# Feed-forward input of a float32 decoder block: product results added onto seeded PSUM banks, and two of four k groups in four column chunks

## The reference

```
h = rms_norm(x, ffn_pre_gain)                    # 256 x 2048
gt, up = split(h @ w_ffn_in)                     # w_ffn_in: 2048 x (2 x 5632)
x = x + rms_norm((silu(gt) * up) @ w_ffn_out, ffn_post_gain)
```

## Time and profile before

| | before |
|---|---|
| median of 3 runs | 1494.03 us (1493.93 to 1494.49) |
| profiled execution, span from first to last instruction | 1491.6 us |
| PE busy | 1481.7 us, 99% |
| DVE busy | 1137.2 us, 76% |
| ACT busy | 835.4 us, 56% |
| weight blocks loaded | 530, 512 KB each |

### The profile page before, as it was taken

One profiled execution on the slowest core, in us unless ns is written; L12 is line 12 of the kernel. 1 busy time (PEld: TensorE's weight loads), 2 busy tenths in 40 slices (PEclk: granted clock), 3 DMA queues, 4 the chain that ended last, 5 costly groups with the idle time before them and its releaser, 6 DMA issues.

```text
span 1491.6 us, 19212 instructions
## 1 busy us (share of the span) xinstructions
PE 1481.7 (99%) x6712; PEld 1220.6 (82%) x6712; DVE 1137.2 (76%) x1353; ACT 835.4 (56%) x1018; POOL 151.4 (10%) x286
## 2 busy tenths in 40 slices
PE   9999999999999999999999999999999999999997
PEld 7888887888888888888888888888888888888886
DVE  6878988855554577657576788888888888887897
ACT  6645455565666544656678455555555555555554
POOL 0000000140220000000000221012222221100000
PEclk9999999999999999999999999999999999999999
DMA  9755555565555655856463666766666667656564
GB/s 342 235 186 178 182 180 186 189 208 187 188 192 171 239 183 185 334 195 211 161 197 116 198 209 221 230 212 216 209 212 199 198 217 236 231 173 213 187 208 169
DMA packets 89859, 305.08 MB, mean 205 GB/s; under 512 B 13056, under 2 KB 13568, under 8 KB 88768
## 3 DMA queue, kind: packets, MB, share of 16 engines
q1 hardware_dynamic: 80144, 285.12, 57.6%
q0 software_dynamic: 9216, 18.63, 3.9%
q10 hardware_dynamic: 432, 0.45, 0.1%
HBM read 294.19 MB, written 2.10 MB: 199 GB/s over the span
## 4 chain that ended last, share of the span: by engine, by line
PE 99%; DMA 0%; DVE 0%; SPq 0%; ACT 0%; issue 0%; DVEq 0%
PE acc L1808 10%; PE acc L1809 10%; PE acc L1810 10%; PE acc L2128 5%; PE acc L2131 5%; PE acc L2130 5%; PE side L2130 5%; PE side L2131 5%; PE side L2128 5%; PE side L1808 4%; PE side L1809 4%; PE side L1810 4%; PE tr L1808 3%; PE tr L1809 3%; PE tr L1810 3%; PE side L2093 2%
## 5 line engine op out<-in xcount | busy, mean ns | idle before, releaser
L548 ACT ACTIVATE w_hi<-raw 128x1024 fp32r<-128x1024 f32 x299 | 315.1, 1060 | 295.4 <-PE acc L2131 90.2
L1001 DVE TENSOR_TENSOR w_lo<-raw,w_hi 128x1024 fp32r<-128x1024 f32 x262 | 320.9, 1227 | 202.0 <-ACT w_hi L529 197.7
L1006 DVE TENSOR_TENSOR w_lo<-raw,w_hi 128x1024 fp32r<-128x1024 f32 x315 | 381.5, 1222 | 102.8 <-ACT w_hi L548 92.9
L529 ACT ACTIVATE w_hi<-raw 128x1024 fp32r<-128x1024 f32 x262 | 276.9, 1059 | 281.3 <-PE acc L1810 165.6
L1808 PE MATMUL acc<-w_hi,xT_hi 128*128 128x512 f32 x504 | 198.3, 393 | 0.5 <-DVE w_lo L1001 0.5
L1810 PE MATMUL acc<-w_hi,xT_lo 128*128 128x512 f32 x504 | 196.3, 389 | 0.0
L1809 PE MATMUL acc<-w_lo,xT_hi 128*128 128x512 f32 x504 | 196.3, 389 | 0.0
L503 POOL DMA_DIRECT2D hT_st<-h_blk x176 | 93.6, 540 | 492.1 <-DVE h_blk L1073 453.6
L1808 PEld LDWEIGHTS acc<-w_hi,xT_hi 128*128 128x128 f32 x504 | 94.6, 188 | 22.6 <-issue 2.6
L1810 PEld LDWEIGHTS acc<-w_hi,xT_lo 128*128 128x128 f32 x504 | 94.6, 188 | 20.0
L1809 PEld LDWEIGHTS acc<-w_lo,xT_hi 128*128 128x128 f32 x504 | 94.7, 188 | 18.9
(11 more groups left out here) (468 smaller groups left out, 2747.3 us busy)
## 6 DMA issues: line engine op xcount, KB each, us to landing
raw<-in_units SPq DMA_DIRECT2D x530, 512.0 KB, 3.9
hT_st<-h_blk POOLq DMA_DIRECT2D x176, 32.0 KB, 1.8
x_tok<-in_x SPq DMA_DIRECT2D x4, 512.0 KB, 5.9
qkT<-qk_blk POOLq DMA_DIRECT2D x64, 32.0 KB, 2.9
xres<-in_x POOLq DMA_DIRECT2D x1, 2048.0 KB, 11.0
m_raw<-in_mem_t POOLq DMA_DIRECT2D x1, 2048.0 KB, 8.6
mq<-in_mem POOLq DMA_DIRECT2D x1, 2048.0 KB, 15.4
x_raw<-in_x_t SPq DMA_DIRECT2D x6, 256.0 KB, 6.4
```

Source lines behind the costliest of these rows:

```text
L529: a_.activation(w_hi[:, j % RING], raw[:, j % RING], ACT.Copy).then_inc(hi_ready, 1)
L548: a_.activation(w_hi[:, v % RING], raw[:, slots[block]], ACT.Copy).then_inc(hi_ready, 1)
L1001: v_.tensor_tensor(w_lo[:, s], raw[:, s], w_hi[:, s].bitcast(F32), ALU.subtract).then_inc(lo_ready, 1)
L1006: v_.tensor_tensor(lo[:, v % RING], raw[:, slot], hi[:, v % RING].bitcast(F32), ALU.subtract).then_inc(lo_ready, 1)
```

## The change

Only the feed-forward input changes (and the numbering of the units behind it: its units are now 280 to 485 and the end is at 595).

- **Pairs per body**: `PAIRS`, 1, 2, 1, 2, 1, 2, 1, 2, 1, 1 for bodies 1 to 10.
- **Order within a body**: block products come first, with three plain up units of the chunk before between them; then that chunk's other up units, and then the body's plain gate units. Chunk 0's last four up units go into body 1.
- **Seeded banks**: products are added by PE onto banks that already hold a partial sum. ACT copies the first product (gate bank 0) into up bank 1, later the sum in up bank 1 into gate bank 1; DVE adds the copy `e_sb` of the second product to up bank 1, once into up bank 0 and once in place. Gate and up results then stand complete in four banks that alternate between two sets from body to body, and silu and the hidden product read them there.
- **Slots**: `raw`'s four slots get four more (`EARLY_SLOTS`, in the place of parts of `hT` not yet written) and two for bodies 2 to 8 (`GROUP_SLOTS`), whose first loads wait for `s_lo` = 2, the second set of activation sums. That set is made in body 1, at its first gate unit.
- **Differences** (`sums`) may be made one or more steps ahead of the product that uses them.

The names of a body's steps: B11, B12, B22, B21 are weight blocks, T1 to T4 the differences of them, in the order made. With two pairs a and b each product step is doubled. Body 4 is units 338 to 361: B11a, B11b, up, T1a, T1b, B21a, B21b, T2a, T2b, up, T3a, T3b, B22a, B22b, up, T4a, T4b, then 3 up and 4 gate units. A one-pair body is B11, up, T1, B21, T2, up, T3, B22, up, T4, and then the other units.

```diff
+PAIRS = (0, 1, 2, 1, 2, 1, 2, 1, 2, 1, 1)
+    rest = [("up", 0, j) for j in range(4, CU)]
+    for i in range(1, 11):
+        k = [[("block", i, g, n) for n in range(4)] for g in range(b.p)]
+        for g in range(b.p):
+            step(k[g][B11])
+        b.p1 = now()
+        t1 = [total(k[g][B11], k[g][B12], k[g][B11], now()) for g in range(b.p)]
+        step(rest[0], 0, t1)
+        for g in range(b.p):
+            step(k[g][B11], t1[g][4])
+        b.p5 = now()
+        t2 = [total(k[g][B11], k[g][B22], k[g][B11], now()) for g in range(b.p)]
+        for g in range(b.p):
+            step(k[g][B21], 0, t2 if g == 0 else ())
+        for g in range(b.p):
+            step(k[g][B11], t2[g][4])
+        b.p6 = now()
+        t3 = [total(k[g][B12], k[g][B22], k[g][B12], 0) for g in range(b.p)]
+        step(rest[1], 0, t3)
+        t4 = [total(k[g][B11], k[g][B21], k[g][B11], b.p6) for g in range(b.p)]
+        for g in range(b.p):
+            step(k[g][B12], t3[g][4], t4 if g == 0 else ())
+        b.p7 = now()
+        for g in range(b.p):
+            step(k[g][B22])
+        step(rest[2])
+        for g in range(b.p):
+            step(k[g][B11], t4[g][4])
...
@@ sync @@
+                elif slot < RING + EARLY_SLOTS:
+                    sp_.wait_ge(x2_ready, 8)
+                else:
+                    sp_.wait_ge(s_lo, 2)
@@ scalar: the loop over a body's splits @@
+                    if v == b.first and i > 1:
+                        gate_silu(i - 1)
+                    if v == b.p1 - 1:
+                        act.wait_ge(unit_used, b.p1)
+                        a_.activation(up_bank(i, 1), gate_bank(i, 0), ACT.Copy).then_inc(u2_seeded, 1)
+                    if v == b.p5 - 1:
+                        a_.activation(e_sb[:], gate_bank(i, 1), ACT.Copy).then_inc(p5_copied, 1)
+                    if v == b.p7 - 1:
+                        a_.activation(gate_bank(i, 1), up_bank(i, 1), ACT.Copy).then_inc(gate1_seeded, 1)
+                    if v == b.blocks - 1 and i > 1:
+                        hidden_hi(i - 1)
+                    if v == b.blocks and i == 1 and max(PAIRS) > 1:
+                        s_hi_part(1)
+                    split_late(v + RING)
@@ vector: the loop over a body's splits @@
+                    if v == b.p6 - 1:
+                        dve.wait_ge(unit_used, b.p6)
+                        dve.wait_ge(p5_copied, i)
+                        v_.tensor_tensor(up_bank(i, 0), up_bank(i, 1), e_sb[:], ALU.add).then_inc(up0_seeded, 1)
+                    if v == b.p7 + 1:
+                        dve.wait_ge(gate1_seeded, i)
+                        v_.tensor_tensor(up_bank(i, 1), up_bank(i, 1), e_sb[:], ALU.add).then_inc(up1_seeded, 1)
+                    if v == b.blocks:
+                        if i > 1:
+                            hidden_lo(i - 1)
+                        hidden_product(i - 1)
+                        if i == 1 and max(PAIRS) > 1:
+                            x_sums(1)
+                    if v == b.blocks + 2:
+                        if i == 1 and max(PAIRS) > 1:
+                            x_sums_lo(1)
+                        hidden_turn(i)
+                    split_late(v + RING)
@@ tensor: the loop over bodies @@
+                for g in range(b.p):
+                    late_product(v + g, gates_[0], *x_block(g, 0, 0), g == 0)
+                if i > 1:
+                    pe.wait_ge(up1_seeded, i - 1)
+                late_unit(v, before, b.up[0][2])
+                pe.wait_ge(s_lo, b.p)
+                for g in range(b.p):
+                    late_product(v + g, gates_[1], *sum_of(S_hi[g], S_lo[g], 0), g == 0)
+                pe.wait_ge(u2_seeded, i)
+                for g in range(b.p):
+                    late_product(v + g, gates_[0], *x_block(g, 1, 0), False)
+                for g in range(b.p):
+                    late_product(v + g, ups[1], *sum_of(S_hi[g], S_lo[g], 1), False)
+                late_unit(v, before, b.up[1][2])
+                pe.wait_ge(up0_seeded, i)
+                for g in range(b.p):
+                    late_product(v + g, ups[1], *sum_of(S_hi[g], S_lo[g], 2), False)
+                for g in range(b.p):
+                    late_product(v + g, ups[0], *sum_of(S_hi[g], S_lo[g], 3), False)
+                late_unit(v, before, b.up[2][2])
+                pe.wait_ge(gate1_seeded, i)
+                for g in range(b.p):
+                    late_product(v + g, gates_[1], *x_block(g, 1, 1), False)
...
```

More of the change, by code:

```diff
@@ L60 @@
 G_S5, G_PRE, G_PROJ, G_MID, G_GLU, G_GATE, G_BR, G_OUT, G_MK, G_XQ, G_MV, G_XO, G_FI, G_FO = (
-    0, 1, 4, 12, 13, 15, 23, 35, 39, 40, 41, 42, 46, 68)
+    0, 1, 4, 12, 13, 15, 23, 35, 39, 40, 41, 42, 46, 47)
 T_GLU, T_BR, T_X1 = 0, 2, 10
-FI_SPLITS, FO_SPLITS, FO_LAST = 19, 53, 56
-S_FI, S_FO, S_END = 284, 474, 583
-def late_units():
[L69 to L80, removed]
-        for _ in range(count):
[L82 to L100, removed]
@@ L101, in late_units @@
     for count in (12, 8, 4):
-        plain(count)
-        pair()
-    plain(8)
+        out_plain(count)
+        out_pair()
+    out_plain(8)
     for count in (4, 8, 4, 4):
[L106 to L119, removed]
+        out_plain(count)
+        out_pair()
+    out_plain(8)
+    first, last = {}, {}
@@ L122 @@
+    plan = {}
+    for n, (key, t, sums) in enumerate(steps):
+        plan[S_FI + n] = place[key] + (t, [tuple(place[k] for k in a[:3]) + a[3:] for a in sums])
+    return loads, plan, bodies, s_fo, now()
+LATE_LOADS, LATE_STEPS, BODIES, S_FO, S_END = late_units()
 N_X, N_GM, N_Y1, N_MEM, N_X1, N_Y2, N_X2, N_Y3 = range(8)
@@ L929, in ffn_in @@
[L929 to L944, removed]
@@ L949, in _ @@
+            for v in range(BODIES[9].end, S_FO):
+                if v == BODIES[9].end:
+                    gate_silu(10)
+                split_late(v + RING)
             preload(3, ACT.Sqrt)
@@ L2148, in out_plain @@
+            pe.wait_ge(up1_seeded, 10)
+            for j in range(2 * BODIES[9].p, CU):
+                late_unit(BODIES[9].end + j - 2 * BODIES[9].p, [up_bank(10, h) for h in range(HALVES)], j)
             def out_plain(q, count, n, g, begins=(None, None), last=False):
@@ L2234 @@
             k0, k1 = 2 * plain[2 * g], 2 * plain[2 * g + 1]
-            order += [left[k0:k1], right[k0:k1]] + blocks_of(left, right, g)
-        order += [left[2 * end:], right[2 * end:]]
+            outs += [left[k0:k1], right[k0:k1]] + blocks_of(left, right, g)
+        outs += [left[2 * end:], right[2 * end:]]
+    for n, block in enumerate(_np.concatenate(outs)):
+        late["out", n] = block[None]
+    order += [late[key] for key, slot, splits in LATE_LOADS]
     def turned(a):
```

359 lines of the change are left out of this document (222 added, 137 removed).

## The result

| | before | changed |
|---|---|---|
| median | 1494.17 us (4 runs) | 1524.01 us (4 runs, 1522.75 to 1525.42) |
| profiled execution, span | 1491.6 us | 1520.8 us |
| PE matmuls | 6712 | 6688 |

The ratio is 1.0199, with a 95% interval of 1.0185 to 1.0214: slower by 29.8 us, where 22 were forecast; 1524.01 lies in the range of 1504 to 1526.

The account below looks back on a forecast made before the run. PE's matmul count was taken as the bound, with DVE's queue setting the pace in dense stretches. Dense bodies 18.0, one-pair bodies 4.0, body 2's one-off 5.2, less 5.4 saved, gave +21.8 us: 1516 us, range 1504 to 1526.

Parts of the forecast that it names:

- The path and its cover: Whole kernel: the path is PE's matmul count at 0.2267 us each while splits arrive in time, with 0.6 us to spare.
- The saving: Feed-forward bodies: four more pairs, each replacing 48 matmuls by 42, take 5.44 us off PE.
- Dense bodies: Two-pair bodies: PE loses 4.51 us each ahead of T3 in three waits; four such bodies, 18.0 us.
- Split to difference 1.26: DVE queue: a difference starts 1.26 us after the start of the split before it.
- Difference to the next 1.27: DVE queue: a difference starts 1.27 us after the start of the difference before it.
- One-pair bodies: Bodies 3, 5, 7, 9 and 10: PE reaches T3 0.80 us late in each, 4.0 us in all.
- Body 2: Body 2: loads held for the second activation sums add 5.2 us to its own 4.5, making 9.7 us.
- Body 1: Body 1: no silu before it, so it loses nothing.
- The output part: Output part: old plan of splits and loads, with the last body's sums off DVE; nothing changes there.
- The spreading works: Rival, bodies: plain units between products let DVE regain its lead, PE never waits; 1488.6 us, chance 0.08.
- No change: Rival, dense bodies: waits of about 1.3 us each eat the gain; 1494 us, chance 0.04.
- The clock: Rival: granted clock falls to 1.2 GHz after each dense body's long wait, adding 10.9 us; 1526.8 us, chance 0.08.

Follow-up runs that it names:

- two spread kernels that move the differences: Changed kernel with later group slots, up units spread wider and differences made at the last up unit before their product: 1489.23 us; also without a difference's subtrahend wait: 1488.87 us.
- later group slots: Changed kernel with the plan taking the two group slots only from unit 295 on, so body 2's first blocks take other slots: 1516.72 us.
- two traces with one wait fewer: Changed kernel, and the spread kernel with moved differences, each without a difference's wait for its subtrahend's landing: 1524.40 us and 1488.87 us.
- spread only: Changed kernel with up units spread wider (2, 2, 2 in two-pair bodies; 2, 1, 1 in body 1) and group slots later, differences not moved: 1499.67 us.
- the seed twice: Changed kernel with DVE making the add that seeds up bank 0 twice in each body: 1535.78 us.
- later silu: Changed kernel with ACT's two silu halves moved from a body's first step to one step after T3: 1522.74 us.

## Why the prediction was right, and where it was off

**The path and its cover.** Right: PE bounds the kernel while the splits arrive in time, and the dense products use that time up. The changed kernel's PE keeps its 0.2267 us outside the waits, and taking the differences off DVE restores it (the run without them).

**The saving.** Right: -5.4 by count, and -4.8 and -5.2 in the two spread kernels that move the differences, with no wait of PE left in the bodies.

**Dense bodies.** Right in mechanism and place; 4.87 against 4.51, and bodies 3 and 4 together took 88.63 us, 5.7 over the 82.96 where 5.3 was said. The three waits (0.42, 1.24, 2.36 in brackets; by the starts about 0.7, 1.5 and 2.6) are the forecast 0.4, 1.5, 2.6. Two steps of the chain were mis-sized. "Split to difference 1.26" stands in it once ahead of a held difference and is now 1.42 (0.20 idle in the rows above): a difference stands behind four semaphore waits and not two, of which one is for the split just before it; with one of the others removed the step is 1.31. "Difference to the next 1.27" stands in it three times and was misread: the earlier trace rows have 886.18 - 884.85 = 1.33, and the changed kernel's rows have 1.35 and 1.36. Together that is 0.4 us a dense body.

**One-pair bodies.** Right, 0.79 against 0.80. That ACT's silu is part of this chain is shown by the run that moved it.

**Body 2.** The mechanism is right (later group slots take 8.2 us away), the size was 9.7 against 13.1. Two terms fell short. The waits themselves took 10.8: at the body's head PE lost 0.7 and not 1.9, but the fifth load of the burst, put at 10.3 us after the first issue by the median landing and 1.49 us a load, was later. The landings of the burst ran to 15.2 us at most, and the difference that needs this load began at 866.37, 12.2 us after the issue at 854.19. The other term is the clock: the rival that was held at 0.08 for every dense body came true here, once, for 2.4 us. A granted clock below 1.00 was among the signs named for being wrong; it did not touch the other bodies of this execution.

**Body 1.** "Body 1 has no silu before it and loses nothing" is the step that failed. ACT is busy until 812.9 with the squares of the norm, loads an activation table from 813.81 to 815.09, and then does chunk 0's two silu halves; the first split behind them starts late, so fewer splits are in hand than the ring allows when the products begin:

```profile
815.11 1.26 ACT L1009 ACTIVATE silu_g<-acc,rstd 128x512 f32<-128x512 f32 x2
816.26 1.06 ACT L641 ACTIVATE w_hi<-raw 128x1024 fp32r<-128x1024 f32 x1
```

PE had finished the unit that this split waits for at 812.42 (809.70 + 2.72). The kernel before has the same lateness in its timeline of ACT:

```profile
816.73 1.06 ACT L535 ACTIVATE w_hi<-raw 128x1024 fp32r<-128x1024 f32 x1
```

There plain units followed, and it cost nothing. In the changed kernel DVE then runs with hardly a gap from the split at 817.35 to the seed, which ends at 833.40; among these instructions is the first `S_lo` (820.99 to 822.21), 1.14 us that the prediction put nowhere. Without a wait PE would have been at T3 at 831.46. The spread kernels have one more up unit in body 1's first gap: a wait of 0.28 at the add is left in the one, none in the one that moves the differences too.

**The output part.** "Nothing there" was wrong by 1.2 us. The code of a difference is shared, and the output part's own dense pairs, with as little to spare as before, now wait. The two traces with one wait fewer are down to 0.6 and 0.7. But the same stretch, with the same code, took from 238.90 us (group slots later) to 240.56 (spread only), and late loads hold a difference in some of them. So how much the waits cost there, and how much the loads, stays open.

**The rivals.** *The spreading works* needed losses below 5.4 us, and PE lost 34.6; that it can work is shown by the kernel that spreads wider and moves the differences. *No change* needed 1.3 us a dense body, against 4.87. *Seeded banks*, the rival of the experiments: refuted, since all of them are in place in kernels whose PE waits nowhere in the bodies. *The clock*: part of the truth, in body 2 here, and in one or three dense bodies of three variants.

The forecast came 8 us short. All rows of the table that missed, but for the 0.5 ahead of the feed-forward part, missed the same way, so the range held it by its width, with 2 us to its end, and not because errors cancelled.

## What to carry to other kernels

An average of free time on an engine (DVE was 75% busy) tells nothing of a stretch where the work is dense and the buffer ahead of it is short: count, for each stretch, the instructions of every in-order queue up to the next instruction that the bound engine needs, and the lead with which it enters. The same instructions a few steps later, and two load slots taken later, made the difference between +2.0% and -0.3%. When a helper gets more waits, look at every place that calls it, and when a load must wait for something late, look at what stands behind it in its queue.

## What the runs showed of the hardware that was not expected

- The granted clock of TensorE fell in mid-run after waits. After 5.8 us of idling 12 matmuls took 5.08 us; in the variant with the seed twice it fell after 3.1 us in three bodies, and did not in a fourth. With the shorter waits it is not settled by their length alone: after idles of 1.24 and 2.36 us the changed kernel's body 4 went on at full pace, while the kernel with the later silu, after 1.14 and 2.35, ran eight or nine matmuls at half of it. The kernel with later group slots did both in one execution: after 1.22 to 1.24 and then 2.32 to 2.36 us it kept its pace in three dense bodies and lost 1.4 us in the fourth. The Trainium skill ("TensorE: Matmul & The Clock Gate", "What's actually happening") has the default state throttled and activity releasing it; the trace agrees in direction, with the clock column at 0.50. So what a repair saves can be given back by the clock, as with the later silu. Whether the spread of the changed kernel's own runs (1522.75 to 1525.42) comes from this was not tried.
- Semaphore waits that were met already were not always free on DVE. Where a difference also waits for the split just before it, it started 1.42 us after that split with four waits in all, 1.31 with three, and 1.26 with two, in the kernel before. Where that split was not needed, as for T4's first difference (1059.36 to 1060.49 in the rows of body 6), four waits cost nothing: 1.13 us, the pace from split to split.
- DVE's add with its result in PSUM took 0.69 us, the same as into SBUF (0.683). ACT's copy of the same bank took 0.598 us into another bank and 0.598 into SBUF (`e_sb`); out of the up bank it took 0.582 into another bank and, in the kernel before, 0.581 into SBUF. The Trainium skill ("ScalarE: Activation LUTs", "Step-by-step: what each stage is for") says that ScalarE's writes into PSUM are faster than those into SBUF; these copies do not show it, and the 0.09 us tried in the prediction was not there.
